# Rotary halves of the retention group: exchanged by a TensorE matmul and rotated on VectorE instead of GpSimd

## What is computed

```python
def rope(x, pos):
    half = x.shape[-1] // 2
    ...
    x1, x2 = x[..., :half], x[..., half:]
    return jnp.concatenate([x1 * cos - x2 * sin, x1 * sin + x2 * cos], axis=-1)

rq = rope(r_q.reshape(B, T, RET_HEADS, RET_DK), pos)
rk = rope(r_k.reshape(B, T, RET_HEADS, RET_DK), pos) * RET_DK ** -0.5
y_c, S_new = retention(rq, rk, r_v.reshape(B, T, RET_HEADS, RET_DV), ret_S)
```

## Time and profile before

| | us |
|---|---|
| median of 3 runs | 945.2 (944.98 to 945.3) |
| the profiled execution, its own time | 945.3 |
| its span, first to last recorded instruction | 943.5 |
| TensorE busy | 934.3 |
| VectorE busy | 493.3 |
| GpSimd busy | 435.1 |
| ScalarE busy | 203.8 |

### The profile page before, as it was taken

The page is one execution under the profiler, slowest core; times in us unless marked ns, Lnnn a source line. Parts: engine busy times, 40 slices in busy tenths (PEclk is TensorE's granted clock), DMA queues, the critical chain, the costliest instruction groups (busy, mean ns, idle before and its releaser), DMA issues.

```text
span 943.5 us, 14968 instructions
## 1 busy us (share of the span) xinstructions
PE 934.3 (99%) x5766; PEld 819.0 (87%) x5766; DVE 493.3 (52%) x1009; ACT 203.8 (22%) x445; POOL 435.1 (46%) x445
## 2 busy tenths in 40 slices
PE   8999999999999999999999999999999999999998
PEld 6776777877999999999977677777789999999998
DVE  5473645854565656512253555478356565653321
ACT  2223245442100000100031243453320000001001
POOL 6200271033976666676411004703168666666770
PEclk9999999999999999999999999999999999999999
DMA  9842311309554444343443322211464444544421
GB/s 284 227 135 90 92 48 46 93 10 236 145 144 135 135 134 135 124 156 124 121 130 109 104 66 66 69 52 51 77 191 134 134 135 136 144 136 135 132 90 45
DMA packets 159314, 112.06 MB, mean 119 GB/s; under 512 B 10118, under 2 KB 157228, under 8 KB 159116
## 3 DMA queue, kind: packets, MB, share of 16 engines
q1 hardware_dynamic: 154660, 104.50, 38.2%
q0 software_dynamic: 3952, 5.85, 2.3%
q10 hardware_dynamic: 632, 0.75, 0.3%
HBM read 108.82 MB, written 2.27 MB: 118 GB/s over the span
## 4 chain that ended last, share of the span: by engine, by line
PE 97%; DVE 1%; DMA 1%; ACT 0%; issue 0%; SPq 0%; DVEq 0%; ACTq 0%
PE ps L1124 51%; PE ps L767 20%; PE ps L1081 7%; PE ps L1142 2%; PE ps L876 1%; PE ps L848 1%; PE ps L977 1%; PE ps L913 1%; PE ps L1020 1%; PE ps L1029 1%; PE ps L795 1%; PE ps L815 1%; DMA arena<-in_x_sample 1%; PE ps L952 1%; PE ps L960 1%; PE ps L1062 0%
## 5 line engine op out<-in xcount | busy, mean ns | idle before, releaser
L767 PE MATMUL ps<-hT,ring 128*128 128x320 f32 x672 | 187.9, 435 | 2.2 <-DVE hT L1593 1.7
L767 PEld LDWEIGHTS ps<-hT,ring 128*128 128x128 f32 x672 | 124.5, 190 | 55.7 <-DVE hT L1593 3.9
L603 POOL TENSOR_TENSOR work<-ring 128x512 f32<-128x512 f32 (+1 forms) x66 | 81.8, 1239 | 155.4 <-issue 113.3
L1124 PE MATMUL ps<-mixT,ring 128*128 128x160 f32 x672 | 105.0, 299 | 0.0
L1124 PE MATMUL ps<-hT,work 128*128 128x160 f32 x672 | 98.5, 299 | 0.0
L1124 PE MATMUL ps<-hT,ring 128*128 128x160 f32 x672 | 98.1, 299 | 0.0
L1124 PEld LDWEIGHTS ps<-mixT,ring 128*128 128x128 f32 x672 | 95.8, 190 | 0.0
L1124 PEld LDWEIGHTS ps<-hT,ring 128*128 128x128 f32 x672 | 93.7, 190 | 0.3
L1124 PEld LDWEIGHTS ps<-hT,work 128*128 128x128 f32 x672 | 93.7, 190 | 0.0
L605 POOL TENSOR_TENSOR work<-ring 128x512 f32<-128x512 f32 (+1 forms) x66 | 82.4, 1249 | 5.2
L604 POOL TENSOR_TENSOR ring<-ring 128x512 f32<-128x512 f32 (+1 forms) x66 | 82.2, 1246 | 5.2
(11 more groups left out here) (393 smaller groups left out, 1361.8 us busy)
## 6 DMA issues: line engine op xcount, KB each, us to landing
ring<-in_w_gu SPq DMA_DIRECT2D x88, 512.0 KB, 5.1
ring<-in_w_in SPq DMA_DIRECT2D x44, 512.0 KB, 4.8
ring<-in_w_down SPq DMA_DIRECT2D x32, 512.0 KB, 4.5
ring<-in_w_out SPq DMA_DIRECT2D x16, 512.0 KB, 4.4
ring<-in_w_down SPq DMA_DIRECT2D x16, 384.0 KB, 3.5
cst<-in_consts POOLq DMA_DIRECT2D x1, 1664.0 KB, 13.2
ring<-in_w_in SPq DMA_DIRECT2D x2, 640.0 KB, 5.7
wqb<-in_mla_wq_b POOLq DMA_DIRECT2D x2, 384.0 KB, 6.8
```

The source lines that it names most:

```text
L603: step(tt(s3, a11, a21, ALU.subtract))
L767: ins = mm(bank(use, 0, T, m), w[:, k, c:c + m], hT[:, k, 0:T], start=(k == 0), stop=(k == KT - 1))
L1124: ins = mm(bank(use, at * HT, HT), left, right(k), start=(opens and k == 0 and at == 0), stop=(closes and k == n - 1), skip_group_check=True)
```

## The change

A table `swap` is added, a 128x128 matrix of zeros and ones that exchanges neighbouring blocks of 32 partitions. TensorE multiplies each raw tile by it, into a PSUM bank of its own (`swap_halves`, names `rqs0`, `rqs1`, `rks0`, `rks1`). VectorE multiplies that bank by the sine table and does the rest of `rotate`, which moves from GpSimd's program to VectorE's: the queries between `queries(2)` and `maxima(2)`, the keys between `convolve(0)` and `maxima(3)`. The four new names enter the turn of banks 0 and 1 around `lx0` and `lx1`. Group C's values, turned before and after `lx0` till now, are both turned after it, and ScalarE's two `value_copy` move behind `conv_input(0)`.

```diff
+    put("swap", (i[:, None] == (i[None, :] ^ 32)))
...
-    fill = [("rv1",), ("rvt0", "lx0", "rvt1"), ("lx1",), ("rg0",)]
+    fill = [("rv1",), ("rqs0", "lx0", "rqs1", "rvt0", "rvt1"), ("rks0", "lx1", "rks1"), ("rg0",)]
...
-                def rotate(n):
-
-                    p = n % 2
-                    t2 = dmx[:, 0:T]
-                    need(pool, "raw_c", l, 4, n + 1)
-                    for q in range(4):
-                        to, of = slice(32 * q, 32 * q + 32), slice(32 * (q ^ 1), 32 * (q ^ 1) + 32)
-                        step(nc.gpsimd.tensor_copy(t2[to], raws[n][of]))
-                    step(nc.gpsimd.tensor_tensor(t2, t2, C("sin_f"), ALU.mult))
-                    step(nc.gpsimd.tensor_tensor(raws[n], raws[n], C("cos_f"), ALU.mult))
...
-                    if grp == "c":
-                        if l == 0:
-                            pool.wait_ge(sem("tables_loaded"), 16 * (len(SMALL[5::2]) + 1))
-                        need(pool, "decay_d", l, H)
-                        wait_filled(pool, f"ds{H - 1}", l)
-                        for n in range(4):
-                            rotate(n)
...
+                def swap_halves(which, n):
+
+                    u = f"{which}{n % 2}"
+                    claim(pe, u, l)
+                    need(pe, "raw_c", l, 4, n + 1)
+                    fill(mm(bank(u, 0, T), C("swap"), raws[n], start=True, stop=True), u)
+
...
-                        value_tiles("rv", l, 0)
+                        swap_halves("rqs", 0)
                         feature("lx0", l, "lx", 0, P)
-                        value_tiles("rv", l, 1)
+                        swap_halves("rqs", 1)
+                        for p in range(2):
+                            value_tiles("rv", l, p)
                     elif h == 2:
+                        swap_halves("rks", 2)
                         feature("lx1", l, "lx", P, P)
+                        swap_halves("rks", 3)
...
-                value_copy("rv", "c", 0)
                 conv_input(0)
-                value_copy("rv", "c", 1)
+                for p in range(2):
+                    value_copy("rv", "c", p)
...
+                def rotate(n):
+
+                    u = ("rqs0", "rqs1", "rks0", "rks1")[n]
+                    p = n % 2
+                    wait_filled(dve, u, l)
+                    t2 = dmx[:, 0:T]
+                    step(v.tensor_tensor(t2, bank(u, 0, T), C("sin_f"), ALU.mult), bank_read=(u, l))
+                    step(v.tensor_tensor(raws[n], raws[n], C("cos_f"), ALU.mult))
+                    if n < 2:
+                        for a in range(2):
+                            rs = slice(a * HD, (a + 1) * HD)
+                            step(v.tensor_tensor(qh[rs, 2 * p + a, :], raws[n][rs], t2[rs], ALU.add),
+                                 "rq_ready" if a else None)
+                    else:
+                        step(v.tensor_tensor(kf[:, p, 0:T], raws[n], t2, ALU.add), "rk_ready")
+
                 def carry_c():
 
-                    need(dve, "rq_ready", l, 2)
...
                 queries(2)
+                rotate(0)
+                rotate(1)
                 maxima(2)
                 b_out(1)
                 queries(3)
                 convolve(0)
+                rotate(2)
+                rotate(3)
                 maxima(3)
```

More of the change, by code:

```diff
@@ L656, in _ @@
                 now_made(pool, "b_out")
-                def rotate(n):
-                    p = n % 2
-                    t2 = dmx[:, 0:T]
-                    need(pool, "raw_c", l, 4, n + 1)
-                    for q in range(4):
-                        to, of = slice(32 * q, 32 * q + 32), slice(32 * (q ^ 1), 32 * (q ^ 1) + 32)
-                        step(nc.gpsimd.tensor_copy(t2[to], raws[n][of]))
-                    step(nc.gpsimd.tensor_tensor(t2, t2, C("sin_f"), ALU.mult))
-                    step(nc.gpsimd.tensor_tensor(raws[n], raws[n], C("cos_f"), ALU.mult))
[L667 to L673, removed]
-                for grp in "dc":
-                    if grp == "c":
-                        if l == 0:
-                            pool.wait_ge(sem("tables_loaded"), 16 * (len(SMALL[5::2]) + 1))
-                        need(pool, "decay_d", l, H)
-                        wait_filled(pool, f"ds{H - 1}", l)
-                        for n in range(4):
-                            rotate(n)
+                for grp in "dc":
                     for h in range(H):
```

## The result

| | before | changed |
|---|---|---|
| median, us | 945.25 (4 runs, 944.98 to 946.97) | 950.85 (4 runs, 950.45 to 951.0) |
| profiled execution, us | 945.3 | 950.9 |
| its span, us | 943.5 | 949.1 |

The ratio of after to before is 1.0054, with a 95% interval of 1.0039 to 1.0068. The change costs 5.6 us. The forecast was 950.5, slower; it held. In several kernels single executions are 1.5 to 2.3 us longer than the rest, like the one at 946.97 here, and a median of few can carry that.

What follows compares the result with a forecast made beforehand. TensorE, busy 934.3 of 943.5 us, was taken as the bound. Head 1's 1.56 us and head 2's 1.08 make 2.64 in each layer, 5.3 in both, giving 950.5 us from 945.2; range 949.2 to 952.0.

Steps and rivals of the forecast that it cites:

- TensorE as the bound: Whole kernel: TensorE, busy 934.3 of 943.5 us, sets the time; work taken from GpSimd is worth nothing by itself.
- The split between busy and idle: TensorE, both layers: some 4.3 us more busy and some 1.0 us more idle.
- The price of a swap: TensorE, heads 1 and 2: each of eight swap matmuls costs 0.54 us, 4.3 us in all, with nothing hiding it.
- The wait of the transposes for ScalarE: Head 1: the first value transposes wait for ScalarE to read `lx0`'s bank, 0.48 us idle on TensorE in each layer.
- VectorE's cover: Heads 1 and 2: VectorE takes 13.7 us of rotations without delaying TensorE; bank free 0.8 us before `rks1`, `maxima(3)` 1.5 early.
- the short values of the earlier trace: Head 2 on VectorE: with GpSimd's rotations gone, the convolution takes 0.45 + 1.73 us; the uncertain term.
- rival 2: Head 2: VectorE is late and `rks1` waits for `rotate(2)`, 0.6 us in each layer, so 951.7 us; chance 0.13.
- The first, no wait for ScalarE: Head 1: transposes start right behind `rqs1`, only the swaps are paid, 949.5 us; chance 0.10.
- The third: Heads 1 and 2: swaps run at the pace of transposes, 0.27 us each, so 948.9 us; chance 0.04.
- The fourth: Stage of the change: TensorE runs freer without GpSimd's reads, giving 945 to 947 us; chance 0.03.
- The sum: Both layers: 1.56 us at head 1 plus 1.08 at head 2, 2.64 in each layer, 5.3 in both.

Runs made afterwards that it cites:

- e9: e4 with VectorE reading both query swaps out of PSUM first and doing the rest of both rotations afterwards; 951.53 us, ratio 1.006.
- e3: Changed kernel without swap matmuls: VectorE exchanges halves by copies, value transposes as before, last rotation behind group A's gates; 945.18 us, ratio 0.9995.
- e10: Changed kernel with the edits of e6 and e8 together; 948.52 us, ratio 1.003.
- e5: Changed kernel with GpSimd kept busy by copies and SBUF multiplications into a scratch tile nobody reads; 952.02 us, ratio 1.0066.
- e8: Changed kernel with value transposes moved to both sides of `rg0` at head 3, ScalarE's value copies behind `exponentials(3)`; 949.3 us, ratio 1.0038.
- e4: Changed kernel reordered at head 1: both query swaps, first value transposes, `lx0`, second ones; value copies before and behind `conv_input(0)`; 953.87 us, ratio 1.0087.
- e6: Kernel before, with group D's output transposed ahead of `weigh_values(0)` and read by VectorE right behind `maxima(1)`; 943.9 us, ratio 0.9982.
- e2: Kernel before, with both value transposes behind `lx0` and ScalarE's value copies behind `conv_input(0)`, no swap or rotation moved; 946.75 us, ratio 1.0014.
- e1: Kernel before plus four swap-table matmuls in each layer whose results nobody reads, rotations still on GpSimd; 950.17 us, ratio 1.0048.

## Why the prediction was right, point by point

**TensorE as the bound.** Right. In the other ten kernels the distance of the median from that of before is twice the change of TensorE's stage, within 0.4 us (0.7 in e9); e3 moved 23 us onto VectorE and 40 us off GpSimd for no change at all. The split between busy and idle was forecast as 4.3 and 1.0 us and came as 5.0 and 0.6: a row of TensorE reaches past its place in the stream and hides a part of the wait behind it (last section), and the first swap is longer.

**The price of a swap,** 0.54 us. Right: 0.54 for three of the four in the changed kernel and for all four in e10. (The four instructions of the earlier trace rows are the parts of two matmuls, so 1.08 us for two was read rightly.) Only the first swap after the wait for bank 0 took 0.65, as the first transposes there had taken 0.39 for 0.32 before. I had carried that extra for the transposes and forgotten it for the swap. These 0.11 us in each layer are the largest term that was missed.

**The wait of the transposes for ScalarE,** 0.48 us. It was 138.64 - 138.17 = 0.47, where 138.17 is the end of `rqs1`'s 0.54. The start of the transposes was put at 138.45 and came at 138.64, with 0.1 from before the stage and 0.1 from the first swap.

**VectorE's cover.** The changed kernel's VectorE at heads 1 to 3:

```profile
138.44 0.49 DVE L1870 TENSOR_TENSOR work<-ps,cst 128x320 f32<-128x320 f32 x1 [2.83 <-PE ps L978]
...
146.29 0.45 DVE L1922 TENSOR_SCALAR wqb<-arena,cols 128x323 f32<-128x323 f32 x1
146.77 1.74 DVE L1924 SCALAR_TENSOR_TENSOR wqb<-arena,cols,wqb 128x323 f32<-128x323 f32 x3
148.54 0.49 DVE L1870 TENSOR_TENSOR work<-ps,cst 128x320 f32<-128x320 f32 x1
...
153.85 1.54 DVE L1899 TENSOR_REDUCE arena<-ps 128x1 f32<-128x128 f32 x3 [1.51 <-PE ps L1007]
```

The convolution took the short values of the earlier trace rows, 0.45 + 1.74, in both layers. `rotate(2)` had read its bank at 149.03, 0.96 us before `rks1` started at 149.99; with the 0.11 from a read to TensorE's start that is 0.85 of cover (0.8 was forecast), and `maxima(3)` waited for its scores with 1.51 us of cover (1.5 forecast). This was the step with the widest choice, and e5 shows what the other end of it would have been: 0.5 us in each layer with GpSimd busy, where rival 2 had 0.6, though in the first layer only half of it at the swap. The rule of the Trainium skill ("SBUF — State Buffer", Who interferes with whom) gave the same answer as the rows, and e5 agrees with it: products with two operands in SBUF slow down beside GpSimd (0.51 to 1.14 us for the 0.49 of L1871), and the product with one in PSUM does not. The convolution's first product reads one tile and a column of scalars, and was slowed too, to 1.12 us from 0.45 in the second layer of e5; the sentence that the forecast drew on, on two SBUF inputs, does not cover it.

**The rivals.** The first, no wait for ScalarE, is refuted by the list of waits; e8 is what it would have looked like, at 949.3 for its 949.5. The second did not come, since no swap waits for a rotation in the list. The third falls with the 0.54. The fourth falls with e3: GpSimd is as free there and TensorE's stage has the same length.

**The sum.** 2.64 us in a layer were forecast and 2.75 measured; 0.1 in all lies ahead of the stage. 5.3 against 5.6.

## What to carry to other kernels

With one engine busy for 99% of the span, as here, an exchange of partitions by matmul was paid in full, and freeing an engine that nobody waits for paid nothing. If such an exchange has to leave GpSimd, an engine with idle stretches can do it with plain copies (e3). When a bank is shared in turn, look at what is queued in front of the instruction that reads it: reading both results first and working on them later was worth 1.5 us in each layer (e9 against e4). And the one wait that the list showed on the busy engine in this stage was a place to win something (e6).

## What the runs showed that I had not expected

**The idle time in a row of TensorE is less than what the wait costs.** The wait for bank 0 stands at 0.41 us in the earlier trace rows, but from the query transposes to the value transposes are 0.90 us before (131.68 to 132.58) and 0.32 in e6, so 0.58 came back. The new wait stands at 0.30 and cost 0.47, that of e2 at 0.51 and cost 0.67. In all three the difference is 0.16 to 0.17 us, the part of the last matmul that reaches past its place in the stream. Distances between starts are the measure.

**The same projection took 4.31 us at some places and 4.41 at others.** It took 4.31 behind a swap in the changed kernel, and 4.41 behind the waits of e2 and e4, behind two swaps in e1, behind the transposes in e9, and at head 3 in the kernel before. The weight loads tell the two apart. At head 2 of the changed kernel the load for `lx1` (first row) starts 0.27 us ahead of its matmul at 145.68; in e1 (second row) it waits for VectorE to give the bank back and starts together with the matmul, at 145.77:

```profile
145.41 4.23 PEld L743 LDWEIGHTS ps<-hT,ring 128*128 128x128 f32 x16
145.77 4.07 PEld L768 LDWEIGHTS ps<-hT,ring 128*128 128x128 f32 x16 [0.36 <-DVEq L435]
```

It starts with the matmul in the other slow cases too, and at the swap that takes 0.65 (132.68). So a bank that comes back late can cost a tenth before TensorE itself is seen idle: in e1 the list of waits has no entry for `lx1`. At head 3 of the kernel before no row names what holds the load. No run was made to test this reading.

**The profiled executions of e4 and e9 lost 1.4 us early.** Their `chunk_scores(1)` starts at 127.97 us, that of the changed kernel at 126.54. The busy times of e9 from 16 to 30 us, with a granted clock of 0.88, and those of the kernel before in the same stretch, with 1.00 (e4 has 0.88 too):

```profile
16.00:30.00 14.00, 13.59 (x44) 8.29 (x43) 6.00 (x14) 2.62 (x6) 11.66 (x20) 0.88 1.06 285
```

```profile
16.00:30.00 14.00, 13.59 (x51) 8.04 (x50) 6.79 (x17) 3.40 (x8) 11.88 (x20) 1.00 1.06 282
```

TensorE was as busy in both, and got through 44 records instead of 51. At full speed 1.00 is 2.4 GHz, and 0.88 as a mean over 14 us would be some 3.4 us at the half speed of 1.2 GHz. That would cost 1.7 us, which is an estimate from this row. It happens in the first projections, far from the change; why in these two and not in the others is open. A comparison of a few tenths of a per cent has to look at where the time was lost.
